# Expert layers rebuilt: two weight blocks on the two column halves, down blocks in pairs, plain fp32 scatter of 64 rows

## The reference

```python
def grouped_moe(x, router_w, router_b, w_gate, w_up, w_down):
    ...
    y = jnp.zeros_like(t)
    for e in range(N_EXPERTS):
        h = jax.nn.silu(t @ w_gate[e]) * (t @ w_up[e])
        y = y + combine[:, e:e + 1] * (h @ w_down[e])
    return y.reshape(B, S, D)
```

## Time and profile before

| | us |
|---|---|
| median of 3 runs (1838.47 to 1840.29) | 1839.88 |
| the profiled execution, its own time | 1839.47 |
| its span in the profile | 1837.7 |
| first expert unit of layer 0 to the end of its last one | 454.7 to 934.3 |
| the same in layer 1 | 1295.9 to 1814.3 |
| PE busy, share of the span | 93% |
| DVE busy, share of the span | 40% |
| ACT busy, share of the span | 26% |

### The profile page before, as it was taken

One profiled execution on the slowest core, in us unless ns is written; L12 is line 12 of the kernel. 1 busy time (PEld: TensorE's weight loads), 2 busy tenths in 40 slices (PEclk: granted clock), 3 DMA queues, 4 the chain that ended last, 5 costly groups with the idle time before them and its releaser, 6 DMA issues.

```text
span 1837.7 us, 20577 instructions
## 1 busy us (share of the span) xinstructions
PE 1715.4 (93%) x8007; PEld 1011.8 (55%) x8007; DVE 738.9 (40%) x1024; ACT 485.0 (26%) x637; POOL 51.0 (3%) x30
## 2 busy tenths in 40 slices
PE   6999999986999999999969999994999999999995
PEld 5888786864344444343438877782535344443352
DVE  5444236545133333241365464547224132333235
ACT  4333335332111111111135353323211111111112
POOL 1000000002000000000022000002000000000000
PEclk9999799997999999999979999996999999999988
DMA  9553323560999999999946565353799999999982
GB/s 374 204 191 129 111 96 133 211 234 28 414 421 408 421 421 400 422 398 423 421 185 252 183 229 183 138 190 130 294 421 405 422 421 404 422 417 402 421 361 92
DMA packets 76660, 543.58 MB, mean 296 GB/s; under 512 B 8625, under 2 KB 9169, under 8 KB 11170
## 3 DMA queue, kind: packets, MB, share of 16 engines
q1 hardware_dynamic: 74610, 530.64, 72.3%
q0 software_dynamic: 1968, 11.82, 1.7%
HBM read 540.33 MB, written 2.10 MB: 295 GB/s over the span
## 4 chain that ended last, share of the span: by engine, by line
PE 90%; DVE 6%; ACT 2%; issue 1%; DMA 1%; POOL 0%; SPq 0%; DVEq 0%; ACTq 0%
PE bank L964 39%; PE bank L612 9%; PE bank L614 9%; PE bank L613 9%; PE bank L955 5%; PE bank L904 4%; PE bank L936 4%; PE bank L956 3%; PE bank L736 2%; PE bank L858 1%; DVE route L1759 1%; PE bank L809 1%; DVE small L1506 1%; DVE X L1530 1%; DMA w_land<-in_ev_w_in 1%
## 5 line engine op out<-in xcount | busy, mean ns | idle before, releaser
L964 PE MATMUL bank<-w_all,xg 128*64 128x512 f32 x2112 | 475.0, 597 | 1.9 <-DVE xg L1862 1.0
L612 PE MATMUL bank<-w_hi,T_hi 128*128 128x512 f32 (+1 forms) x800 | 313.5, 392 | 20.6 <-DVE w_lo L1483 18.1
L614 PE MATMUL bank<-w_hi,T_lo 128*128 128x512 f32 (+1 forms) x800 | 311.6, 390 | 0.0
L613 PE MATMUL bank<-w_lo,T_hi 128*128 128x512 f32 (+1 forms) x800 | 311.6, 390 | 0.0
L1483 DVE TENSOR_TENSOR w_lo<-w_land,w_hi 128x2048 fp32r<-128x2048 f32 (+1 forms) x96 | 214.3, 2240 | 223.3 <-ACT w_hi L1148 223.3
L964 PEld LDWEIGHTS bank<-w_all,xg 128*64 128x64 f32 x2112 | 143.2, 137 | 270.0 <-issue 267.1
L964 PE MATMUL bank<-w_all,hT 128*64 128x512 f32 x1056 | 256.2, 609 | 7.2 <-issue 6.2
L1148 ACT CAST w_hi<-w_land 128x2048 fp32r<-128x2048 f32 (+1 forms) x100 | 184.4, 1854 | 267.3 <-PE bank L614 260.8
L1910 DVE SCALAR_TENSOR_TENSOR X<-bank,weight,X 128x512 f32<-128x512 f32 x264 | 185.2, 743 | 84.7 <-PE bank L956 84.7
L1900 DVE TENSOR_TENSOR y_lo<-bank,y_hi 128x512 fp32r<-128x512 f32 x132 | 91.3, 692 | 292.7 <-ACT y_hi L1339 292.7
L612 PEld LDWEIGHTS bank<-w_hi,T_hi 128*128 128x128 f32 x800 | 153.7, 192 | 51.8 <-issue 19.1
(11 more groups left out here) (245 smaller groups left out, 1142.7 us busy)
## 6 DMA issues: line engine op xcount, KB each, us to landing
w_all<-in_moe_w_gate SPq DMA_DIRECT2D x132, 1024.0 KB, 12.1
w_all<-in_moe_w_up SPq DMA_DIRECT2D x132, 1024.0 KB, 11.9
w_all<-in_moe_w_down SPq DMA_DIRECT2D x132, 1024.0 KB, 13.0
w_land<-in_ev_w_in SPq DMA_DIRECT2D x32, 1024.0 KB, 5.0
w_land<-in_od_w_in SPq DMA_DIRECT2D x32, 1024.0 KB, 4.9
w_land<-in_ev_w_out SPq DMA_DIRECT2D x16, 1024.0 KB, 4.9
w_land<-in_od_w_out SPq DMA_DIRECT2D x16, 1024.0 KB, 4.8
w_land<-in_att_w SPq DMA_DIRECT2D x7, 1024.0 KB, 4.7
```

Of the source, the lines that this page charges most:

```text
L612: pe.matmul(dst, hi_l, hi_r, start=start, stop=False)
L613: pe.matmul(dst, hi_l, lo_r, start=False, stop=False)
L614: return pe.matmul(dst, lo_l, hi_r, start=False, stop=stop)
L964: ins = pe.matmul(dst[r, :], cols(c), w[:, c, :], start=start and c < 2, stop=stop and c >= 2)
```

## The change

- Gate and up of an expert go through one bank: in each step PE takes one gate unit and one up unit (`two_units`), gate on rows 0 to 63 of bank 0 and up on rows 64 to 127. Nothing is left to fold. `turn` turns the one copy `gu_s` with 64 x 64 pieces of the identity, gate to bank 6 and up to bank 7.
- Down units go in pairs, again one on each column half, so a bank holds two finished blocks of 512 output columns. ACT copies it once as fp32 (`y_s`); `y_hi`, `y_lo` and the subtraction on DVE are gone.
- `scatter` is four fp32 matmuls for a pair of blocks: 64 rows of `placeT` and of `y_s` each, into banks 4 to 7.
- An expert's down units now stand after the next expert's gate and up units. SP fetches gate and up units in turn. `used` rises by two after each pair of units.
- `gather` uses banks 1 to 3 in turn instead of four banks and stands after all down units of the third expert; the token counts are copied from bank 3 to `hot` first. Each step of the first expert of a quad waits only for its own part of `xg`.
- The statistics at a layer's end are taken four blocks at a time.

```diff
             def gather(Q, n):
+                for q in range(8):
+                    if q >= 3:
+                        pe.wait_ge((xg_out_a, xg_out_v)[(q - 3) % 2], 4 * Q + (q - 3) // 2 + 1)
...
-                        dst = bank[(0, 5, 6, 7)[q % 4]][:, c * 4 * CAP:c * 4 * CAP + n * CAP].rearrange("p (e s) -> p e s", e=n)
+                        dst = bank[1 + q % 3][:, c * 4 * CAP:c * 4 * CAP + n * CAP].rearrange("p (e s) -> p e s", e=n)
...
+                    def two_units(pos, dst, cols, start, stop):
+
+                        for h in range(2):
+                            pe.wait_ge(*U.landed(q, pos + h))
+                        for c in range(4):
+                            for h in range(2):
+                                ins = pe.matmul(dst[halves[h], :], cols(c), U.weights(q, pos + h)[:, c, :],
+                                                start=start and c == 0, stop=stop and c == 3)
+                        ins.then_inc(used, 2)
...
+                    def turn(e):
+
+                        E = 4 * Q + e
+                        pe.wait_ge(gu_out, E + 1)
+                        ge(pe, acc_done, 8 * (E - 1))
                         for c in range(4):
+                            for h in range(2):
+                                ins = pe.matmul(bank[6 + h][:, c * CAP:(c + 1) * CAP], gu_s[halves[h], c * P:(c + 1) * P],
+                                                const[halves[h], halves[h]], start=True, stop=True)
+                        ins.then_inc(turned, 1)
...
-                            pe.matmul(dst[:], cols, y_hi[:, n % 2, :], start=True, stop=False)
-                            pe.matmul(dst[:], cols, y_lo[:, n % 2, :], start=False, stop=True).then_inc(scat_fill, 1)
+                    def scatter(e, p):
                         E = 4 * Q + e
+                        pe.wait_ge(y_out_done, 2 * E + p + 1)
+                        ge(pe, acc_done, 8 * E + 4 * p)
                         for a in range(TT):
+                            for h in range(2):
+                                pe.matmul(bank[4 + 2 * a + h][:], placeT[halves[h], e % 2, a * P:(a + 1) * P],
+                                          y_s[halves[h], p, :], start=True, stop=True).then_inc(scat_fill, 1)
...
+                    def down(pos, e, following):
+
+                        E = 4 * Q + e
+                        pe.wait_ge(h_done, E + 1)
+                        for p in range(2):
+                            ge(pe, y_out_done, 2 * E + p - 1)
+                            two_units(pos + 2 * p, bank[2 + p], lambda c: hT[:, c, :], True, True)
+                            if p == 0 and following is not None:
+                                turn(following)
+                                slots(following)
...
+                        up_gate(12 * e, e, lambda: None if first and e == 1 else scatter(e - 2, 1))
+                        down(12 * e + 8, e - 1, e)
+                        if e < 3:
+                            first_sums(e - 1, e)
...
+                        act.copy(y_s[:, p, :], bank[2 + p][:]).then_inc(y_out_done, 1)
...
-                        dve.tensor_tensor(y_lo[:, n % 2, :], bank[3 + n % 2][:], y_hi[:, n % 2, :], ALU.subtract) \
-                            .then_inc(y_lo_done, 1)
```

More of the change, by code:

```diff
@@ new lines, in body @@
+                    for e in range(4):
+                        if e == 0 and first:
+                            slots(0)
+                            up_gate(0, 0)
+                            silu(0)
+                            continue
+                        up_gate(12 * e, e)
+                        down(12 * e + 8, e - 1, e)
+                    if not last or layer:
+                        tokens_out(Q + 1, 1 if last else 4)
+                    if last and layer:
+                        up_gate(48, 4)
+                        down(56, 3, 4)
+                        down(60, 4, None)
+                    elif last:
+                        down(48, 3, None)
@@ L1811, in route_tokens @@
                 dve.wait_ge(rank_ready, layer + 1)
+                chain.wait()
                 one_hot(rank[:, :, 0:4], 4)
@@ new lines, in down @@
+                    def down(e, following, n=0):
+                        if following is not None:
+                            product(following)
+                        if n:
+                            places(n)
+                    n = 0 if last and not layer else 1 if last else 4
+                    for e in range(4):
+                        if e == 0 and first:
+                            product(0)
+                            continue
+                        if not (first and e == 1):
+                            add(e - 2, 1)
+                        if e == 1:
+                            weights(0)
+                        down(e - 1, e, n if e == 3 else 0)
+                        if e < 3:
+                            add(e - 1, 0)
@@ new lines, in body @@
+                    if n:
+                        tokens_out(Q + 1, n)
+                    add(2, 0)
+                    if last and layer:
+                        add(2, 1)
+                        down(3, 4)
+                        add(3, 0)
+                        add(3, 1)
+                        weights(4)
+                        down(4, None)
+                        add(4, 0)
+                        statistics(4, 0)
+                        add(4, 1)
+                        statistics(4, 1)
+                    elif last:
+                        add(2, 1)
+                        down(3, None)
+                        add(3, 0)
+                        statistics(3, 0)
+                        add(3, 1)
+                        statistics(3, 1)
```

458 lines of the change are left out of this document (189 added, 269 removed).

## The result

| | before | after |
|---|---|---|
| median, us | 1839.43 | 1829.76 |
| lowest to highest, us | 1838.47 to 1840.29 | 1828.17 to 1831.12 |
| span of the profiled execution, us | 1837.7 | 1829.3 |

The kernel before has four runs here and had three ahead of the prediction, so its median moved from 1839.88 to 1839.43. The ratio is 0.9947, with a 95% interval of 0.9930 to 0.9964. The change makes the kernel 9.7 us faster. The forecast was 46: the sign was right, the size was not, and 1829.76 lies outside 1786 to 1820.

What follows compares the result with a forecast made beforehand. PE bounds the kernel, with transfers close behind capping any saving. Layers win 23.5 and 29.3 us, tails and routing lose 6.3: 46.5 us off 1839.47 gives 1793.0, 1793.5 as median; range 1786 to 1820.

Steps and rivals of the forecast that it cites:

- PE per expert, 26.6 us: PE's work for one expert after the change: units, two scatters, turn and slots sum to 26.6 us, 1.65 less than 28.25.
- rival B: In scatters the two row halves work one after another: an expert takes 29.9 us, the kernel 1897 us, slower; chance 0.07.
- rival A: Row halves overlap only in part or array shape changes cost more: scatter matmuls 1.3 times, expert 27.6, 1818 us; chance 0.30.
- The product is done some 1.5 us after turn: DVE's product in each expert: ready 1.5 us after turn, hidden because PE has a pair of 3.44 us before needing it.
- The prediction's last paragraph: Signs of a wrong forecast: PE waits for DVE's adds, or granted clock under 1.00 inside stretches beyond the last gather.
- The transfers as a cap: Weight transfers at 2.49 us a unit set layer 0's end: last landing 907.2, end 910.8 against 934.3, 23.5 us won.
- Layer 1 as the later of two sums: Layer 1's end: PE 1784.4 against transfers 1781.9, PE barely setting it; 1785 against 1814.3, 29.3 us won.
- some waits for both: Layer 1's end: allowance for waits that takes PE's 1784.4 to 1785.
- The tails, +3.1 us twice: Each layer's end, last unit to end of layer norm statistics: 12.0 us instead of 8.85, 3.1 us more, twice.
- The second scatter's wait for four adds: Layer 1's seventeenth pass puts two scatters of one expert together; the second waits 1.9 us for four adds.
- The gathers: Gather inside a layer: same 64 matmuls, right behind a pair whose copy must be out (0 to 0.9 us), so 9.3 us.
- rival C: PE, waiting for transfers in later quads, loses its clock: 5 us each, two to ten give 1803 to 1843; chance 0.05.

Runs made afterwards that it cites:

- e5: The kernel of e1 with 512 KB in place of 1 MB for each unit after a layer's first twelve; 1776.3 us, one run.
- e7: The kernel before with 512 KB in place of 1 MB for each unit after a layer's first twelve; 1842.3 us, one run.
- e1: The changed kernel with two buffers for `hT`, by the parity of the expert, and without the product's wait on `y_out_done`; 1816.06 us, ratio 0.9879.
- e16_e1_again: The kernel of e1 run once more, unchanged; 1813.64 us, ratio 0.9859.
- e8: The kernel of e1 with the loads of the layer norm's gain and bias held until the layer's last expert unit has landed; 1812.6 us, ratio 0.9864.
- e6_after_half: The changed kernel with 512 KB in place of 1 MB for each unit after a layer's first twelve; 1831.2 us, one run.
- e2_h_after_unit: The changed kernel with its single `hT`, the product waiting for PE's last down pair and not for ACT's copy of it; 1814.62 us, ratio 0.9867.

## Why the prediction was wrong, point by point

**PE per expert, 26.6 us: right as work, wrong as time.** Row halves run at once: 1.92 us for the eight records, and with the 0.15 us that the pair before them takes over 3.44, 2.07 us where the prediction had 2.18. The turn takes 1.04 where it had 1.13, the slots 0.37 where it had 0.45. e5 measures 26.3 us. With it falls rival B. For two row halves the trace has 3.44 / 1.92 = 1.8, and what is missing to 2 is mostly one way in and out for each scatter, so rival A's factor does not show. The Trainium skill's 3.07 in "TensorE: Matmul & The Clock Gate", section "Measured speedup vs the span model", is for four row tiles, and no run here has four.

**"The product is done some 1.5 us after turn": the step that failed first.** It looked at what the product needs, gate and up turned, and not at what it overwrites. `hT` was single before too, but the product needed no wait for it: the down units of the expert before had all been done by then. The change makes the product's input between the two down pairs of the expert before, and gives it the new wait on `y_out_done`. Measured: the product ends at 618.48, 5.0 us behind the turn (613.44) and not 1.5, and PE idles for up to 1.33 us, 24 times. With two buffers the product ends 0.88 us behind the turn. The price is 30.6 us of waits, 12.6 us more at gathers and, with the clock, 12 us: 55 us of PE's time in the two layers. The prediction had 61.1 us of saving on PE there (31.2 + 29.9), and PE alone saves 66.0 (32.4 + 33.6, e7 less e5), so this one wait took five sixths of it. Of the 11 us that were left the tails took 3.1; the two spans differ by 8.4, which is that within the 4 us that one profile leaves open. The prediction's last paragraph named DVE's adds and a low clock as signs of being wrong: the low clock came, but the wait was for DVE's product.

**The transfers as a cap: right in kind, and 10 us too early in layer 0.** The cap was not reached by the changed kernel, so this step did no harm to the number, but it would have: e1, without the failed wait, is at 1814 to 1816, not at 1793. Of these 21 to 23 us, 10 are this step in layer 0 and 13 or more the next one in layer 1. The pitch of 2.49 us for a unit was right. Missing was what else uses the DMA engines: in e1, 5.0 us for gain and bias at the end, 3.8 us in smaller gaps, and 1.6 us at the start. From the 13th landing to the last a unit of layer 0 takes 2.54 us on average. The kernel before has the same average (454.5 us for 179), but not for this reason: 2.54 is PE's own pace there (121.85 us for 48 units), and gain and bias are asked for at 923.2, when the last unit has landed. So its trace does not show this loss; it comes only when PE, and with it GpSimd's loads, are early enough to meet the last units.

**Layer 1 as the later of two sums: the wrong form.** 488.4 us for PE and 485.9 for the transfers gave 489 with "some waits for both". PE alone was even 4 us better than that (484.3 in e5). But the end is the last landing that is waited for plus all of PE's work behind it, 442 + 60.4. With two bounds this close the sum must be made at the worst cut, and the worst cut is just ahead of a long piece of work that needs no weights. It is worth 13 us in e1 and 16 in e16_e1_again.

**The tails, +3.1 us twice: half right.** +2.8 in layer 1; +0.3 in layer 0, where a blocked operation of DVE in the kernel before hid the difference. The earlier trace rows stop at the statistics; the 2.62 us stand in the next row of the trace. The second scatter's wait for four adds, put at 1.9 us, is 2.12 us.

**The gathers** were to take 9.3 us with up to 0.9 of waiting; in the changed kernel the wait was 2.62 us and went, in four of six gathers, with a fall of the clock. That is rival C in a place where I had not put it: behind a wait for DVE and not for transfers, at 1.7 us each.

## What to carry to other kernels

For each step that a change puts into a tight chain, list what it overwrites as carefully as what it reads: a single buffer turned a saving of 66 us of PE's time into 11. Where two resources are within a few per cent of each other, find the last wait for the one and add all the work of the other behind it, since the later of the two sums is too low. And before a tail is shortened, look at what the freed engine will meet there.

## What the runs showed of the hardware that I had not expected

- A longer queue of weight transfers (up to eleven under way against seven) changes neither their order nor their pitch: 2.486 us for 1 MB whether it lands 13 or 23 us after its issue.
- A 1 MB load that broadcasts a row to all partitions, on another queue, costs the weights beside it about a full unit each: two of them put 4.6 to 5.0 us into the landings, and e8 took them out again.
- An operation on 128 x 2 elements can take 4.48 us: DVE waits for the end of GpSimd's running instruction, and again for the next one.
- 2.6 to 2.8 us of idle PE ahead of a gather inside a layer went together with 3.4 us at the 1.2 GHz level in it, in six of six such gathers of e6_after_half and four of six of the kernel after. In e2_h_after_unit, with 2.0 us of waiting there, it was none of six, and in e1_two_h, with 0.7 to 0.8 us, none.
